# Natural feature order for the rows of the second norm, with strided reads by TensorE's transposes

## The chip, the cores and the metric

The kernel runs on one core of a Trainium2 chip. The metric is the device time of one execution in microseconds (us); the times before are the median of three runs. The engines are called as the profile calls them: PE is TensorE's matmul, PEld its weight load, DVE VectorE, ACT ScalarE, POOL GpSimd, SP SyncE.

## The reference, cut to what matters

One layer of a backbone: a mixing part (convolution and retention heads), then a channel part, a mixture of experts. What this change touches lies between the two. For each of the 640 tokens (128 context, 512 latent):

```python
x = x + g1 * m
xn = rmsnorm(x, norm_ffn_g) * (1 + sc2) + sh2
lg_group = t @ w_rg + b_rg          # t = xn as rows of 1024 features
lg_exp = t @ w_re + b_re            # top-1 group, then top-2 experts in it
hid = silu(t @ w1e) * (t @ w3e)     # for each of 32 experts
acc = acc + ge[:, None] * (hid @ w2e)
x = x + g2 * acc                    # then a last rmsnorm
```

All data is float32. A feature's place in a row of xn is free, as long as the router's and the experts' weights meet it in the same order.

## The kernel before, in words

The tokens are five tiles of 128 (tile 0 the context). `P` is 128, `D` is 1024, `KT` is 8, `NT` is 5. Each engine runs a program of its own, in the order in which it is written; semaphores join them.

**Weights and feature order.** The router's and the experts' weights lie in memory with the feature as the outer index and are loaded by "(p k) n -> p k n": partition p holds the eight features 8p to 8p+7, so that each partition gets one long piece. For step k of a product over the features, the stationary operand must therefore hold features k, 8+k, 16+k and so on. In the kernel before, DVE writes the normalised row `xn2[t]` in that order: `second_norm(t)` (lines 1568 to 1580) reads x in natural order and writes with 128 words from one element to the next, so that each block of 128 words is one k.

**Routing stage (295 to 403 us).** For each tile PE runs the output projection in two halves (`project`, line 1137), and between them the transposes of the tile before (`router_T`, line 1145: eight transposes, each loads a 128 x 128 block of `xn2` as the stationary operand), then `router` (L1154), `ranks` (L1164, L1165) and `slots` (L1174) of earlier tiles. DVE adds the residual, runs `second_norm` (L1572 to L1580; its multiplication is L1578, its addition goes through the helper at L1356), `choose` and `place`. ACT squares the rows and copies the transposes out of PSUM (L867). POOL writes every `xn2` tile to memory (`expert_in_rows`, L629).

**Expert stage (403 to 660 us).** POOL gathers the rows of two experts, 64 each, into `xe` (L633); PE transposes them (`rows_T`, L1244, eight transposes for a pair of experts, four of them in each expert's turn); DVE copies them to `xeT` (L1678). Each expert: `gate_up` (L1252, L1256), `hidden_T` (L1262), `down` (L1272). The transposes of a pair's rows stand one pair ahead, between `hidden_T` and `down` of the expert before.

**Loads of the experts.** SP loads 3 MB for each expert into five slots. The first loads wait for the output projection's two last halves (a slot becomes free), the fourth expert's for all `expert_in_rows` writes, the fifth's for the first two gathers, and every later one for the `gate_up` and `down` five experts earlier (L461, L462, L465). 

The last stage (660 to 694 us) reads both expert results of each token, adds them and normalises.

Of the kernel before, what the change touches and what calls it, by code (L numbers as in the profile page):

```python
# [7 lines left out]
P = 128  # L8
D = 1024
KT = D // P  # L10
# [61 lines left out]
ALU = mybir.AluOpType  # L72
# [59 lines left out]
def layer(nc, a, y_prompt, y_sample, new_f, new_b):  # L132
# [7 lines left out]
    with ExitStack() as ctx:  # L140
        def sb(name, shape, dt=F32):
            return ctx.enter_context(nc.sbuf_tensor(name, shape, dt))

        def sem(name):
            return ctx.enter_context(nc.semaphore(name))

        bank = [ctx.enter_context(nc.psum_tensor(f"bank{b}", [P, SL], F32)) for b in range(8)]
# [14 lines left out]
        x = sb("x", [P, NT, D])  # L162
# [22 lines left out]
        stat = sb("stat", [P, 4, NT])  # L185
# [16 lines left out]
        def k(name):  # L202
            lo, hi = CONSTS[name]
            return kept[:, lo:hi]

        ident = k("ident")
# [3 lines left out]
        q = arena_b[:, 0:2560].rearrange("p (t n) -> p t n", t=NT)  # L210
# [25 lines left out]
        rows = [arena_b[:, 2 * D * c:2 * D * c + 2 * D].rearrange("p (s n) -> p s n", s=2) for c in range(4)]  # L236
# [3 lines left out]
        xn2 = [arena_a[:, D * ((t + 3) % NT):D * ((t + 3) % NT) + D] for t in range(NT)]  # L240
# [13 lines left out]
        def tagged(t, j):  # L254
# [6 lines left out]
        xe = arena_c[:, 0:2048].rearrange("p (b n) -> p b n", b=2)  # L261
# [55 lines left out]
        ssq2_done, ms2_done, root2_done, xn2_ready, xn2T_mm, xn2T_ev, rt_mm, lg_ready = (sem(n) for n in (  # L317
            "ssq2_done", "ms2_done", "root2_done", "xn2_ready", "xn2T_mm", "xn2T_ev", "rt_mm", "lg_ready"))
# [55 lines left out]
        def bank_of(n):  # L374

            return bank[(4 + n) % 8]
# [14 lines left out]
        def conv_bank(piece, g):  # L391

            return bank[4 + g] if piece == 2 else bank[2 * g + piece % 2]
# [521 lines left out]
        def _(pe):  # L915
# [46 lines left out]
            def split_product(out, lhs, rhs, start, stop):  # L962
                pe.matmul(out, lhs[0], rhs[0], start=start, stop=False)  # L963
                pe.matmul(out, lhs[0], rhs[1], start=False, stop=False)  # L964
                return pe.matmul(out, lhs[1], rhs[0], start=False, stop=stop)  # L965


            def conv_step(piece, kt, w):

                for g in range(2):  # L970
                    cols = slice(HALF_TOK * g, HALF_TOK * g + HALF_TOK)
                    last = split_product(conv_bank(piece, g)[:, 0:HALF_TOK], w, [b[:, kt, cols] for b in (xn_hi, xn_lo)],
                                         kt == 0, kt == KT - 1)
                return last
# [27 lines left out]
            for n in range(3, CONV_PIECES):  # L1002
# [4 lines left out]
                for kt in range(KT):  # L1007
                    last = conv_step(n, kt, [b[:, kt, :] for b in w])
# [13 lines left out]
            for piece in range(CONV_PIECES, PIECES):  # L1022
# [3 lines left out]
                for t in range(NT):  # L1026
# [6 lines left out]
                    for c in range(2):  # L1033
                        kt = 2 * j + c
                        last = split_product(bank_of(n)[:, :], [b[:, kt, cols] for b in (xn_hi, xn_lo)],
                                             [b[:, c, :] for b in w], kt == 0, kt == KT - 1)
# [54 lines left out]
            for t in range(NT):  # L1091
# [8 lines left out]
                for h in range(HEADS):  # L1100
                    cols = slice(DH * h, DH * h + DH)
                    last = pe.matmul(bank[3][:, cols], sm[:, cols], v[:, t, cols], start=True, stop=(t == 0))
                    if t >= 1:
                        pe.matmul(bank[3][:, cols], qTf[t % 2][:, cols], sfw[:, cols], start=False, stop=False)
                        last = pe.matmul(bank[3][:, cols], qTb[t % 2][:, cols], sbk[:, t - 1, cols], start=False, stop=True)
# [12 lines left out]
                for h in range(HEADS):  # L1118
                    last = pe.transpose(bank[5][:, P * h:P * h + P], q[:, t, DH * h:DH * h + DH], ident)
# [20 lines left out]
            def router_T(t):  # L1140
                pe.wait_ge(xn2_ready, t + 1)
                for kt in range(KT):
                    if t >= 1 and kt % 4 == 0:
                        pe.wait_ge(xn2T_ev, 2 * t - 1 + kt // 4)
                    last = pe.transpose(bank[4 + kt // 4][:, P * (kt % 4):P * (kt % 4) + P], xn2[t][:, P * kt:P * kt + P], ident)
                    if kt % 4 == 3:
                        last.then_inc(xn2T_mm, 1)

# [30 lines left out]
            for t in range(NT):  # L1179
                project(t, 0)  # L1180
                if t >= 1:
                    router_T(t - 1)

                if t == NT - 1:
                    router(t - 1)
                project(t, 1)
                if 1 <= t < NT - 1:
                    router(t - 1)
                if t >= 3:
                    slots(t - 3)  # L1190
                if t >= 2:
                    ranks(t - 2)
# [23 lines left out]

            late_mod(0)
            router_T(NT - 1)
            slots(NT - 3)
            ranks(NT - 2)  # L1220
# [20 lines left out]
            def rows_T(p_, tiles):  # L1241

                for kt in tiles:
                    last = pe.transpose(bank[kt // 4][:, P * (kt % 4):P * (kt % 4) + P], xe[:, p_, P * kt:P * kt + P], ident)  # L1244
                    if kt % 4 == 3:
                        last.then_inc(xe_mm, 1)

# [27 lines left out]

            pe.wait_ge(xe_in[0], 16)
            rows_T(0, range(KT))
            def finish(n):

# [10 lines left out]
            for n in range(EXPERTS):  # L1290
                s, p_, pair = e_slot[n % NSLOT], n % 2, (n // 2) % 2
# [21 lines left out]
            with pe.If(count > 0):  # L1313
# [8 lines left out]
                for n in range(2 * NT):  # L1322
                    mine = tagged_ov[:, n, :].rearrange("p (m two) -> p two m", two=2)
                    for half in range(2):
                        last = pe.matmul(bank[4][BLK * half:BLK * half + BLK, 0:OVB // 2], hit_ov[:, n, :], mine[:, half, :],
                                         start=(n == 0), stop=(n == 2 * NT - 1))
# [19 lines left out]
        def _(dve):  # L1346
            steps = [0]

            def then(ins):

                steps[0] += 1
                ins.then_inc(step, 1)
                dve.wait_ge(step, steps[0])

            def tt(out, in0, in1, op):
                return dve.tensor_tensor(out, in0, in1, op)  # L1356
# [79 lines left out]
            for m in range(CB):  # L1436
                dve.wait_ge(proj_mm, CB + m + 1)
                dve.wait_ge(conv_c_ev, CB)
                for g in range(2):
                    cols = slice(HALF_TOK * g, HALF_TOK * g + HALF_TOK)  # L1440
                    last = tt(u[:, m, cols], u[:, m, cols], conv_bank(CB + m, g)[:, 0:HALF_TOK], ALU.mult)
# [5 lines left out]
            for m in range(CB):  # L1447
                for lo, hi, w in spans:
# [4 lines left out]
                                                  in1=o[:, :, 1:], op0=ALU.mult, op1=ALU.add))  # L1453
                    then(dve.scalar_tensor_tensor(out=o[:, :, 0:w - 1], in0=i_[:, :, 1:], scalar=conv_w[:, 2, m:m + 1],
                                                  in1=o[:, :, 0:w - 1], op0=ALU.mult, op1=ALU.add))
                dve.wait_ge(proj_mm, 2 * CB + m + 1)
                for g in range(2):
                    cols = slice(HALF_TOK * g, HALF_TOK * g + HALF_TOK)
                    last = tt(yconvT[:, m, cols], yconvT[:, m, cols], conv_bank(2 * CB + m, g)[:, 0:HALF_TOK], ALU.mult)
# [11 lines left out]
            for n in range(2 * (NT - 1)):  # L1471
                dst = (q, kk)[n // (NT - 1)]
                t = n % (NT - 1) + 1
# [94 lines left out]
            def second_norm(t):  # L1568
                dve.wait_ge(x1_ready, 2 * t + 2)
                dve.wait_ge(scale2_ready, 1)  # L1570
                dve.wait_ge(ssq2_done, t + 1)
                dve.tensor_scalar(stat[:, 1, t:t + 1], stat[:, 0, t:t + 1], 1.0 / D, EPS, ALU.mult, ALU.add).then_inc(ms2_done, 1)  # L1572
                dve.wait_ge(root2_done, t + 1)
                then(dve.reciprocal(stat[:, 3, t:t + 1], stat[:, 2, t:t + 1]))
                side = min(t, 1)
                as_qk = lambda r: r.rearrange("p (q k) -> p q k", q=P)
                dst = xn2[t].rearrange("p (k q) -> p q k", q=P)
                then(dve.scalar_tensor_tensor(out=dst, in0=as_qk(x[:, t, :]), scalar=stat[:, 3, t:t + 1],  # L1578
                                              in1=as_qk(rows[2][:, side, :]), op0=ALU.mult, op1=ALU.mult))
                tt(dst, dst, as_qk(rows[1][:, side, :]), ALU.add).then_inc(xn2_ready, 1)  # L1580

            def over(ap, n):

# [57 lines left out]
            for t in range(NT):  # L1641
# [9 lines left out]
                if t == 0:  # L1651
                    dve.wait_ge(rows_in[2], 16)
                    dve.wait_ge(gffn_in, 16)
                    for side in range(2):
                        last = dve.scalar_tensor_tensor(out=rows[2][:, side, :], in0=rows[2][:, side, :], scalar=1.0, in1=g_ffn,
                                                        op0=ALU.add, op1=ALU.mult)
# [163 lines left out]
            with dve.If(count > 0):  # L1820
                def ov(ins, n):
# [10 lines left out]
                                            in0=on.rearrange("p (t j) b -> p t j b", j=2)[:, :, 1, :], scalar=float(TOK), in1=second,  # L1832
                                            op0=ALU.mult, op1=ALU.add), 3)
# [6 lines left out]
                                         op1=ALU.add).then_inc(idx_ov_ready, 1)  # L1840
# [9 lines left out]
                for m in range(OVB // 2 - 1):  # L1850
                    with dve.If(count > m):
# [6 lines left out]
                        for j in range(2):  # L1858
# [4 lines left out]
                                                        scalar=g_ctx_ov[:, 2 * m + j:2 * m + j + 1], in1=gate_row[:, j, :],  # L1863
                                                        op0=ALU.mult, op1=ALU.add), 11 + 4 * m + 2 * j)
# [58 lines left out]
```

## Time and profile before

| | |
|---|---|
| time, median of three runs | 697.33 us (695.92 to 697.91) |
| profiled execution | 695.76 us, span 693.9 us |
| PE busy | 586.9 us (85%) |
| DVE busy | 311.8 us (45%) |
| ACT, POOL busy | 140.3 us, 145.3 us |
| bytes moved by DMA | 178.67 MB, mean 257 GB/s |

The span is the time from the first to the last instruction of the profiled execution; 1.86 us lie around it. The page cuts the span into 40 slices of 17.35 us. A chain of waits is the work that ended last, followed back from the end. A group of instructions is one line, engine, operation and shape. A releaser is what ended an engine's idle time.

### The profile page before, as it was taken

What the parts mean: (1) busy time and instruction counts of PE and PEld (TensorE: products, weight loads), DVE (VectorE), ACT (ScalarE), POOL (GpSimd) and SP (SyncE); (2) the same over time, 40 slices, a digit from 0 to 9 for tenths busy, and PEclk for the clock granted to TensorE, in tenths of its full rate; (3) what the DMA queues carried; (4) which work ended last, traced back from release to release, by engine and by line L of the source; (5) the groups of instructions that cost most, each with busy time, mean ns of one, the idle gap of its engine ahead of it and who ended that gap; (6) DMA issues with size and microseconds to landing.
All of it is one profiled execution on the core that took longest, in us unless ns stands there. A gap on an engine that the chain in (4) does not pass through costs nothing.

```text
span 693.9 us, 8564 instructions
## 1 busy us (share of the span) xinstructions
PE 586.9 (85%) x3496; PEld 394.9 (57%) x3496; DVE 311.8 (45%) x619; ACT 140.3 (20%) x269; POOL 145.3 (21%) x113
## 2 busy tenths in 40 slices
PE   3799999999999989899999758999888877788800
PEld 3579999888888856544554425555444433443300
DVE  1432228623602357524677636665433333334347
ACT  5334531121322333301111120111000100000012
POOL 0043642424242100020000021232222222121200
PEclk9999999999999999999999669999988999999955
DMA  7985231130330399770006899999999999999484
GB/s 276 387 296 200 71 122 53 69 122 0 122 116 6 124 369 328 256 289 30 31 31 231 361 347 400 363 422 419 419 419 420 420 419 420 420 420 420 177 317 186
DMA packets 47482, 178.67 MB, mean 257 GB/s; under 512 B 5624, under 2 KB 5800, under 8 KB 34768
## 3 DMA queue, kind: packets, MB, share of 16 engines
q1 hardware_dynamic: 39116, 155.83, 57.0%
q0 software_dynamic: 7360, 19.63, 7.8%
q10 hardware_dynamic: 964, 2.63, 1.1%
q8 instruction: 29, 0.48, 0.3%
q14 instruction: 13, 0.11, 0.0%
HBM read 170.17 MB, written 14.19 MB: 266 GB/s over the span
## 4 chain that ended last, share of the span: by engine, by line
PE 66%; DMA 21%; DVE 6%; ACT 3%; SPq 2%; issue 2%; DVEq 0%; POOLq 0%; ACTq 0%
DMA ring<-in_w_up_e 17%; PE bank L963 9%; PE bank L964 9%; PE bank L1137 9%; PE bank L965 9%; PE bank L1252 9%; PE bank L1272 4%; PE bank L922 3%; PE bank L939 2%; PE bank L1244 2%; PE bank L1154 2%; DMA ring<-expert_out_rows 1%; PE bank L1017 1%; SPq L461 1%; SPq L465 1%
## 5 line engine op out<-in xcount | busy, mean ns | idle before, releaser
L1252 PE MATMUL bank<-ring,arena_ab 128*64 128x256 f32 x416 | 104.5, 409 | 27.5 <-DMA ring<-in_w_up_e 23.7
L1256 PE MATMUL bank<-ring,arena_ab 128*64 128x256 f32 x416 | 104.6, 409 | 0.0
L1252 PEld LDWEIGHTS bank<-ring,arena_ab 128*64 128x64 f32 x416 | 59.7, 148 | 76.4 <-DMA ring<-in_w_up_e 36.8
L572 POOL TENSOR_TENSOR w_lo<-ring,w_hi 128x1024 fp32r<-128x1024 f32 x25 | 61.3, 2452 | 112.6 <-ACT w_hi L723 112.6
L643 POOL DMA_INDIRECT expert_out_rows<-arena_ab,row_out x32 | 40.1, 1254 | 130.4 <-DVE arena_ab L1356 130.4
L1356 DVE TENSOR_TENSOR arena_ab<-arena_ab,bank 64x256 f32<-64x256 f32 x32 | 19.6, 613 | 106.3 <-ACT arena_ab L879 106.2
L963 PE MATMUL bank<-xn_hi,w_hi 128*128 128x320 f32 x192 | 61.6, 321 | 3.7 <-DVE xn_lo L1356 3.6
L963 PE MATMUL bank<-w_hi,xn_hi 128*128 128x512 f32 x160 | 63.3, 396 | 0.0
L964 PE MATMUL bank<-w_lo,xn_hi 128*128 128x512 f32 x160 | 62.9, 393 | 0.0
L965 PE MATMUL bank<-w_hi,xn_lo 128*128 128x512 f32 x160 | 62.8, 392 | 0.0
L1256 PEld LDWEIGHTS bank<-ring,arena_ab 128*64 128x64 f32 x416 | 59.7, 148 | 0.0
L964 PE MATMUL bank<-xn_lo,w_hi 128*128 128x320 f32 x192 | 59.4, 310 | 0.0
L965 PE MATMUL bank<-xn_hi,w_lo 128*128 128x320 f32 x192 | 59.3, 309 | 0.0
L879 ACT ACTIVATE arena_ab<-bank 64x256 f32<-64x256 f32 x32 | 12.0, 376 | 224.6 <-PE bank L1256 224.6
L1272 PE MATMUL bank<-ring,arena_ab 128*64 128x512 f32 x208 | 50.4, 605 | 1.4 <-ACT arena_ab L883 1.4
L723 ACT ACTIVATE w_hi<-ring 128x1024 fp32r<-128x1024 f32 x25 | 26.5, 1062 | 114.1 <-PE bank L965 114.1
L963 PEld LDWEIGHTS bank<-xn_hi,w_hi 128*128 128x128 f32 x192 | 36.5, 190 | 6.7 <-issue 5.0
L1356 DVE TENSOR_TENSOR arena_ab<-bank,arena_ab 128x512 f32<-128x512 f32 x37 | 25.5, 690 | 27.9 <-PE bank L1272 27.8
L1137 PE MATMUL bank<-ring,arena_cd 128*128 128x512 f32 x80 | 36.4, 597 | 1.3 <-ACT arena_ab L847 1.3
L965 PEld LDWEIGHTS bank<-xn_hi,w_lo 128*128 128x128 f32 x192 | 36.6, 191 | 0.0
L964 PEld LDWEIGHTS bank<-xn_lo,w_hi 128*128 128x128 f32 x192 | 36.5, 190 | 0.0
L1137 PE MATMUL bank<-ring,arena_ab 128*128 128x512 f32 x80 | 36.0, 592 | 0.0
(235 smaller groups left out, 903.3 us busy)
## 6 DMA issues: line engine op xcount, KB each, us to landing
ring<-in_w_gate_e SPq DMA_DIRECT2D x26, 1024.0 KB, 26.3
ring<-in_w_up_e SPq DMA_DIRECT2D x26, 1024.0 KB, 28.0
ring<-in_w_down_e SPq DMA_DIRECT2D x26, 1024.0 KB, 26.7
ring<-in_w_ada SPq DMA_DIRECT2D x11, 2048.0 KB, 12.8
ring<-in_w_in SPq DMA_DIRECT2D x6, 2048.0 KB, 8.2
arena_ab<-in_w_gate_e SPq DMA_DIRECT2D x6, 1024.0 KB, 25.8
arena_ab<-in_w_up_e SPq DMA_DIRECT2D x6, 1024.0 KB, 27.5
arena_ab<-in_w_down_e SPq DMA_DIRECT2D x6, 1024.0 KB, 26.2
```

The source lines that it names most:

```text
L572: pool.tensor_tensor(as_piece(w_lo[p_ % 2], p_), piece_of(w, p_), as_piece(w_hi[p_ % 2], p_), ALU.subtract).then_inc(w_lo_ready, 1)
L643: pool.indirect_dma_start(half_rows, bass.IndirectOffsetOnAxis(ap=column, axis=0), ysb[:, p_, :], None, bounds_check=2 * 2 * TOK - 1, oob_ ...
L723: act.activation(as_piece(w_hi[piece % 2], piece), piece_of(w, piece), ACT.Copy).then_inc(w_hi_ready, 1)
L922: last = pe.matmul(out[32 * j:32 * j + 32, :], cs[:, kt, :], w[:, kt, :], start=(kt < 4), stop=(kt >= 4))
L963: pe.matmul(out, lhs[0], rhs[0], start=start, stop=False)
L964: pe.matmul(out, lhs[0], rhs[1], start=False, stop=False)
L965: return pe.matmul(out, lhs[1], rhs[0], start=False, stop=stop)
L1137: last = pe.matmul(bank[n % 4][:, :], lhs, w[:, kt, :], start=(kt == 0), stop=(kt == KT - 1))
L1252: pe.matmul(bank[2 + p_][0:BLK, 0:DE], lhs, w_gate(s)[:, kt, :], start=(kt == 0), stop=(kt == KT - 1))
L1256: last = pe.matmul(bank[2 + p_][BLK:2 * BLK, 0:DE], lhs, w_up(s)[:, kt, :], start=(kt == 0), stop=(kt == KT - 1))
L1272: last = pe.matmul(bank[6 + p_][BLK * half:BLK * half + BLK, :], hidT[:, p_, c, :], w_down(s)[:, c, SL * half:SL * half + SL], start=(c == ...
L1356: return dve.tensor_tensor(out, in0, in1, op)
```

## The change

DVE writes the normalised rows in natural feature order: both of its operations on a tile read and write consecutive words. The rows go to memory and come back by the gather in that order. PE's transposes in `router_T` and `rows_T` take, for step k, every eighth word of a row from word k on, so that the transposed blocks hold what they held before. Nothing else is changed: the number of instructions, the bytes moved and the waits are the same.

```diff
@@ router_T
-                    last = pe.transpose(bank[4 + kt // 4][:, P * (kt % 4):P * (kt % 4) + P], xn2[t][:, P * kt:P * kt + P], ident)
+                    last = pe.transpose(bank[4 + kt // 4][:, P * (kt % 4):P * (kt % 4) + P], xn2[t][:, kt:D:KT], ident)
@@ rows_T
-                    last = pe.transpose(bank[kt // 4][:, P * (kt % 4):P * (kt % 4) + P], xe[:, p_, P * kt:P * kt + P], ident)
+                    last = pe.transpose(bank[kt // 4][:, P * (kt % 4):P * (kt % 4) + P], xe[:, p_, kt:D:KT], ident)
@@ second_norm
                 side = min(t, 1)
-                as_qk = lambda r: r.rearrange("p (q k) -> p q k", q=P)
-                dst = xn2[t].rearrange("p (k q) -> p q k", q=P)
-                then(dve.scalar_tensor_tensor(out=dst, in0=as_qk(x[:, t, :]), scalar=stat[:, 3, t:t + 1],
-                                              in1=as_qk(rows[2][:, side, :]), op0=ALU.mult, op1=ALU.mult))
-                tt(dst, dst, as_qk(rows[1][:, side, :]), ALU.add).then_inc(xn2_ready, 1)
+                then(dve.scalar_tensor_tensor(out=xn2[t], in0=x[:, t, :], scalar=stat[:, 3, t:t + 1],
+                                              in1=rows[2][:, side, :], op0=ALU.mult, op1=ALU.mult))
+                tt(xn2[t], xn2[t], rows[1][:, side, :], ALU.add).then_inc(xn2_ready, 1)
```

## Rows read from the trace of the kernel before

**Rows 1.** Page, 40 slices of the span: DMA share in tenths, GB/s
```profile
DMA  7985231130330399770006899999999999999484
GB/s 276 387 296 200 71 122 53 69 122 0 122 116 6 124 369 328 256 289 30 31 31 231 361 347 400 363 422 419 419 419 420 420 419 420 420 420 420 177 317 186
```

**Rows 2.** Chain of waits, 313 to 435 us: start, duration (us), what
```profile
313.98 2.00 DVE arena_ab L1578
...
351.42 0.87 PE bank L1145 x8
...
382.71 1.98 DVE arena_ab L1578
...
404.04 5.32 DMA arena_cd<-expert_in_rows,idx
...
409.41 1.98 PE bank L1244 x8
...
418.95 0.59 PE bank L1244 x4
...
425.86 2.60 issue
...
434.09 0.59 PE bank L1244 x4
```

**Rows 3.** Timeline: transposes of tiles 0, 2 and 4; idle before and releaser
```profile
317.96 1.09 PE L1145 MATMUL bank<-kept,arena_ab 128*128 128x128 f32 x8 [1.66 <-DVE arena_ab L1356]
...
351.25 0.80 PEld L1145 LDWEIGHTS bank<-kept,arena_ab 128*128 128x128 f32 x7 [0.29 <-issue]
...
386.65 1.57 PEld L1145 LDWEIGHTS bank<-kept,arena_ab 128*128 128x128 f32 x8 [5.49 <-DVE arena_ab L1356]
386.66 1.97 PE L1145 MATMUL bank<-kept,arena_ab 128*128 128x128 f32 x8 [4.58 <-DVE arena_ab L1356]
```

**Rows 4.** Groups by shape, DVE: busy us, mean ns | idle before
```profile
L1578 DVE SCALAR_TENSOR_TENSOR arena_ab<-x,stat,arena_ab 128x1024 f32<-128x1024 f32 x5 | 10.0, 1995 | 0.2
L1356 DVE TENSOR_TENSOR arena_ab<-arena_ab 128x1024 f32<-128x1024 f32 x5 | 9.6, 1919 | 0.2
L1887 DVE SCALAR_TENSOR_TENSOR ring<-x,stat,arena_ab 128x1024 f32<-128x1024 f32 x5 | 6.4, 1284 | 0.5 <-DMA out<-ring 0.4
L1356 DVE TENSOR_TENSOR x<-x,ring 128x1024 f32<-128x1024 f32 x5 | 6.1, 1224 | 0.2
```

**Rows 5.** The same view: sums over 32 words, strided (L1620) and consecutive
```profile
L1636 DVE TENSOR_REDUCE arena_cd<-arena_cd 128x1 f32<-128x32 f32 x10 | 1.9, 186 | 0.3
...
L1620 DVE TENSOR_REDUCE arena_cd<-arena_cd 128x8 f32<-128x32 f32 x5 | 1.0, 206 | 0.2
```

**Rows 6.** Stretches: length, busy us of each engine, granted clock, DMA share, GB/s
```profile
382.00:386.60 4.60, 0.07 (x4) 0.00 (x0) 4.18 (x5) 0.69 (x2) 0.00 (x0) 0.86 1.01 426
386.60:399.00 12.40, 12.34 (x62) 7.97 (x62) 7.20 (x42) 1.78 (x3) 0.53 (x1) 0.50 0.85 336
...
425.80:428.40 2.60, 0.06 (x2) 0.00 (x0) 2.40 (x7) 0.00 (x0) 0.06 (x1) 1.00 0.90 284
430.00:433.00 3.00, 3.00 (x18) 2.10 (x16) 0.27 (x1) 0.00 (x0) 1.18 (x1) 0.50 1.03 429
436.00:438.00 2.00, 2.00 (x20) 1.21 (x18) 1.37 (x3) 0.00 (x0) 0.00 (x0) 1.00 0.34 80
...
452.00:498.00 46.00, 46.00 (x344) 25.52 (x340) 25.07 (x43) 5.22 (x16) 13.22 (x12) 1.00 1.02 420
```

**Rows 7.** Timeline of SP's queue: issues of expert loads
```profile
368.82 0.34 SPq L461 DMA_DIRECT2D ring<-in_w_gate_e  x1
...
436.58 0.33 SPq L465 DMA_DIRECT2D ring<-in_w_down_e  x1
...
468.09 0.33 SPq L465 DMA_DIRECT2D ring<-in_w_down_e  x1
...
474.26 0.33 SPq L465 DMA_DIRECT2D ring<-in_w_down_e  x1
```

**Rows 8.** Line L633, the sixteen gathers of expert rows: time to landing
```profile
DMA to landing us min/median/max: 4.4/8.5/9.8
```

## The prediction

> **What bounds the kernel now.** I read the page's slices first: from the 26th on (about 434 us) the DMA engines are full at 419 to 420 GB/s, up to the 36th or 37th, some 640 us [rows 1]. That is the loading of the experts. One expert is 3 MB, so it takes 3.146 MB / 420 GB/s = 7.5 us; SP's issues, which follow PE's progress, are 6.17 us apart at 468 to 474 us [rows 7]. PE is thus faster than the loads in the middle of the expert stage, and the end of that stage is the time at which the load queue was last empty, plus the bytes that were left. The last such hole is at 436 to 438 us, where the DMA share is 0.34 and 80 GB/s are moved [rows 6]; it ends with the issue at 436.58 us, which waits for PE's `down` of the second expert [rows 7]. So whatever moves the issue at 436.58 us moves the end by as much, and work that PE gains or loses after it, below 7.5 - 6.17 = 1.3 us an expert, moves nothing.
>
> Then the chain of waits up to there. DVE's norm of tile 0 is on it (313.98 us), then PE through the routing stage without a gap that DVE ends (the transposes of tile 2 stand in it as PE's own work), then DVE's norm of tile 4 (382.71), PE, the first gather (404.04, 5.32 us), the eight transposes of the first pair (409.41), four in the first expert's turn (418.95), a pause of PE of 2.60 us at 425.86, and four more at 434.09 [rows 2]. The timeline says how long PE stood: 1.66 us before tile 0's transposes and 4.58 us before tile 4's, both for DVE [rows 3].
>
> **DVE's part, removed.** In the strided form the multiplication takes 1995 ns and the addition 1919 ns. Nearest forms with consecutive words: the last norm's multiplication (same operands, 1284 ns) and an addition of two 128x1024 operands (1224 ns) [rows 4]. A tile gains 711 + 695 = 1406 ns, five tiles 7.0 us. For tiles 1 to 3 it lies beside PE's projections and is worth nothing. For tile 0 it is on the path: PE is ready 1.66 us before DVE, so all of 1.41 us counts. For tile 4 again 1.41 us. Together -2.82 us, the whole gain to be had.
>
> **PE's part, added.** No weight load of the kernel before reads with a stride, so the price must be bounded. What a transpose costs now: the seven weight loads in 0.80 us, each lasting 0.14 us, start (0.80 - 0.14) / 6 = 0.11 us apart [rows 3], and eight transposes take 0.87 us on the chain, 0.109 us each [rows 2]: the transposes go at the pace of their weight loads, with nothing in between to hide a longer load. At the clock of 0.50 at 386.6 to 399 us [rows 6] eight take 1.97 us [rows 3].
>
> [...] Below nothing is excluded, since no word less is loaded. For the other end I take what DVE pays. A sum over 32 words takes 186 ns with consecutive words and 206 ns where every eighth word is read, the stride of this change: 20 / 32 = 0.62 ns a word, though it has eight results instead of one [rows 5]. The norm's two operations give 711 / 1024 = 0.69 and 695 / 1024 = 0.68 ns a word for a stride of 128 words [rows 4]. I take 0.69 ns: 128 words, 0.088 us a transpose. If a strided word has a time of its own and not a surcharge, it is about 1224 / 1024 + 0.69 = 1.9 ns less the fixed part of the operation (186 ns for a sum over 32 words, so some 0.15 us or 0.15 ns a word), 1.7 ns: 0.22 us a transpose, 0.11 us more. So 0 to 0.11 us, and I take 0.088, since two views of DVE agree on it; that PE's port behaves as DVE's is the open point.
>
> [...]
>
> **The sum up to 436.58 us, at 0.088 us a transpose.**
> - Tile 0: DVE -1.41.
> - Transposes of tiles 0 to 3: 32 x 0.088 = +2.82. SP's first expert load (368.82 us [rows 7]) is then issued 1.41 us later.
> - Tile 4: DVE -1.41.
> - Transposes of tile 4: 8 at half clock. A load there has 1.57 / 8 = 0.20 us [rows 3], 1.5 ns a word, close to the 1.7 ns of a strided word, so the surcharge may vanish or stay: 0 to 0.70, I take +0.35. The list of rows to gather is ready at +0.35.
> - The gather runs among loads of the experts that were issued at +1.41. Its 5.32 us are near the shortest of the sixteen, 4.4 us [rows 8], so it follows its own issue more than the queue; between +0.35 and +1.41 I take +0.9.
> - First pair's eight transposes, again at half clock: +0.35.
> - The four at 418.95: DVE copies them out and then works without a pause until PE may go on at 428.46 us: +0.35.
> - The next four (423.41): PE then stands 2.60 us for that DVE work; DVE is busy 2.40 us of it [rows 6]. They are free as long as they cost under 2.60 us.
> - The four at 434.09: +0.35.
>
> Sum +0.9 + 3 x 0.35 = +1.95 us.
>
> **After it.** Four transposes an expert add 0.35 us to 6.17, 6.52 us, still under the loads' 7.5. The last experts have no transposes in their turn, so the end of the stage and the last stage stay. DVE's writes to memory, the gathers and the results are the same bytes. So +1.95 us at the end: the profiled execution of 695.76 us becomes 697.7 us. That execution is 1.57 us under the median of the three runs, 697.33, to which the time below refers: 699.3 us.
>
> With 0 us a transpose: the list is ready at -2.82, the loads come at -1.41, the gather between, and the sum is -2.1 us: 695.2 us. With 0.11 us: 32 x 0.11 - 2.82 = +0.7 at the list, +2.1 at the loads, the gather at +1.4, then little for the eight at half clock and 2 x 0.44: about +2.5 us, 699.8 us. About 0.3% (2.1 us) is what a measurement of this kernel can tell from no change, so the forecast lies just inside.
>
> **The rivals.**
> - *Strided weight loads are free.* For it: nothing in the trace shows PE paying for any pattern, and the load may be paced by the array. Against: DVE pays for reads and for writes alike [rows 4, 5], at a pace of about 1 ns a word, and PE at full clock wants a word every 0.85 ns, faster still. 695.2 us.
> - *A strided load costs more than DVE's surcharge, and the transposes replace DVE as what the routing stage waits for.* The place is the 32 transposes of tiles 0 to 3 between the projections, which no wait covers. It decides from about 0.09 us a transpose, where the sum passes +2.1 us. For it: the 0.11 us pitch leaves a load no slack at all [rows 3]. At twice DVE's price, 0.176 us: the loads at 32 x 0.176 - 1.41 = +4.2, the list at 5.6 - 2.8 + 1.4 = +4.2, then 1.4 + 0.7 + 0.7 for the pairs, +7.0 us: 704.3 us. Only from 1.3 / 4 = 0.33 us a transpose would the whole expert stage go at PE's pace.
> [...]
>
> **How the numbers follow.** Forecast 0.50, free loads 0.28, dearer loads 0.13, clock kept 0.09. The forecast's own bounds (+1 to +2.6 us) and the spread of the three runs (2 us from lowest to highest) put 0.28 of its 0.50 inside 0.3% and 0.22 above. Free loads: 0.16 faster, 0.12 inside. Dearer loads: all slower. Clock kept: 0.04 faster, 0.05 inside. So faster 0.20, within 0.3% 0.45, slower 0.35. The range reaches down to the free loads' time and up to the beginning of the dearer ones, 694.9 to 703.0 us; it leaves out about half of the dearer loads and some of the free ones' spread.
>
> **What the profile after would show.** L1578 near 1.28 us and the addition near 1.22 us; PE's wait before tile 0 near 0.3 us. The weight loads of L1145 at full clock 0.2 us apart and eight transposes in about 1.6 us on the chain (0.87 if they are free). SP's first expert load 1.4 us later (1.4 earlier if free). The hole near 436 us still there, moved by the sum. In the full stretch 452 to 498 us [rows 6] SP's issues 6.5 us apart, DMA still at 420 GB/s. The prediction is wrong if a transpose has another pitch, if DMA no longer fills that stretch, or if the gather doesn't follow the list.

## The result and the profile after

| | before | changed |
|---|---|---|
| time, median of ten runs | 697.13 us (694.75 to 699.27) | 693.79 us (691.96 to 695.06) |
| profiled execution, span | 693.9 us | 692.9 us |
| DVE busy | 311.8 us | 304.9 us |
| PEld busy | 394.9 us | 398.1 us |

The ratio to the kernel before is 0.9948, 95% interval 0.9934 to 0.9963: 3.6 us faster (2.6 to 4.6). The forecast was 699.3 us with a range of 694.9 to 703.0, so the change went the other way and just out of the range. It lies beside the first rival, free strided loads (695.2 us).

DVE first. Groups by shape of the changed kernel, busy us and mean ns of one behind the bars; L1576 and the first L1356 are the norm's multiplication and addition:

```profile
L1576 DVE SCALAR_TENSOR_TENSOR arena_ab<-x,stat,arena_ab 128x1024 f32<-128x1024 f32 x5 | 6.4, 1285 | 0.2
...
L1885 DVE SCALAR_TENSOR_TENSOR ring<-x,stat,arena_ab 128x1024 f32<-128x1024 f32 x5 | 6.4, 1285 | 0.5 <-DMA out<-ring 0.4
...
L1356 DVE TENSOR_TENSOR arena_ab<-arena_ab 128x1024 f32<-128x1024 f32 x5 | 6.1, 1225 | 0.2
```

Both are what the nearest consecutive forms said [rows 4]: 1995 - 1285 = 710 ns and 1919 - 1225 = 694 ns.

Then PE. The timeline of the changed kernel, with the idle time before an operation in brackets: the transposes of tile 0, the weight loads of tile 2 (seven of the eight), the transposes of tile 4:

```profile
316.16 1.15 PE L1145 MATMUL bank<-kept,arena_ab 128*128 128x128 f32 x8 [0.28 <-DVE arena_ab L1356]
...
349.53 0.86 PEld L1145 LDWEIGHTS bank<-kept,arena_ab 128*128 128x128 f32 x7 [0.24 <-issue]
...
385.30 1.97 PE L1145 MATMUL bank<-kept,arena_ab 128*128 128x128 f32 x8 [3.23 <-DVE arena_ab L1356]
```

Against [rows 3]: PE waits 0.28 instead of 1.66 us before tile 0, and 3.23 instead of 4.58 us before tile 4, 1.38 and 1.35 us gained. A weight load lasts 0.19 instead of 0.14 us, but they start (0.86 - 0.19) / 6 = 0.11 us apart, as before. The chain of waits, with start and duration:

```profile
313.56 1.30 DVE arena_ab L1576
...
349.69 0.89 PE bank L1145 x8
...
370.67 8.66 PE bank L1137 x16
...
382.70 1.29 DVE arena_ab L1576
...
402.94 5.15 DMA arena_cd<-expert_in_rows,idx
...
408.14 1.99 PE bank L1244 x8
...
424.95 2.55 issue
```

Eight transposes take 0.89 instead of 0.87 us [rows 2]. The 8.66 us are an accident of the clock (below): the same sixteen products took 6.96 us before. In stretches of the changed kernel (length, busy times, then granted clock, DMA share, GB/s):

```profile
370.70:374.50 3.80, 3.80 (x6) 1.48 (x6) 3.23 (x19) 0.00 (x0) 0.00 (x0) 0.55 1.01 420
...
385.30:398.00 12.70, 12.70 (x63) 7.99 (x63) 7.16 (x41) 1.78 (x3) 0.53 (x1) 0.50 0.99 385
...
429.70:433.10 3.40, 3.40 (x26) 2.06 (x24) 1.29 (x2) 0.65 (x2) 0.51 (x1) 1.00 1.01 419
434.00:436.00 2.00, 2.00 (x22) 1.35 (x20) 1.93 (x4) 0.00 (x0) 0.51 (x1) 1.00 1.00 334
```

The granted clock was 0.50 at 371 to 374 us, where it had been 1.00 before, and 1.00 at 430 to 433 us, where it had been 0.50 [rows 6]. Such stretches fall differently in the two executions. The first cost PE 8.66 - 6.96 = 1.7 us, more than tile 0 had given, so tile 4's norm began no earlier than before (382.70 and 382.71 us). The second gave as much back: PE's pause ended at 427.50 us, 0.96 us earlier than before, and the issue that ended the last hole came earlier by 2.6 us:

```profile
434.00 0.33 SPq L465 DMA_DIRECT2D ring<-in_w_down_e  x1
```

It was at 436.58 us before [rows 7]. That the 2.6 us lie near the two terms of the norm is therefore partly luck of this execution. The last expert's first product came at 647.63 instead of 649.80 us, and the last stage from there took 45.3 instead of 44.1 us; so the spans of the two profiles differ by only 1.0 us, the medians by 3.3 us. The steps below are read from single stages, the gain from the medians.

### The profile page after: what moved, and what is told of

It reads as the page before. It is cut to its first block, busy times and chain, and to the rows that moved or that the text cites. A ratio compares the mean times of both kernels' runs of the same rounds, so it can differ in the third digit from the quotient of the medians.

```text
span 692.9 us, 8564 instructions
## 1 busy us (share of the span) xinstructions
PE 588.9 (85%) x3496; PEld 398.1 (57%) x3496; DVE 304.9 (44%) x619; ACT 140.2 (20%) x269; POOL 145.3 (21%) x113
## 4 chain that ended last, share of the span: by engine, by line
PE 67%; DMA 21%; DVE 5%; ACT 3%; SPq 2%; issue 2%; DVEq 0%; POOLq 0%; ACTq 0%
DMA ring<-in_w_up_e 17%; PE bank L963 9%; PE bank L1137 9%; PE bank L964 9%; PE bank L965 9%; PE bank L1252 9%; PE bank L1272 4%; PE bank L922 3%; PE bank L939 2%; PE bank L1244 2%; PE bank L1154 2%; DMA ring<-expert_out_rows 1%; PE bank L1017 1%; SPq L461 1%; PE bank L1086 1%
## 5 line engine op out<-in xcount | busy, mean ns | idle before, releaser
L1356 DVE TENSOR_TENSOR arena_ab<-arena_ab,bank 64x256 f32<-64x256 f32 x32 | 19.4, 607 | 103.8 <-ACT arena_ab L879 103.7
L1137 PE MATMUL bank<-ring,arena_cd 128*128 128x512 f32 x80 | 38.1, 621 | 1.3 <-ACT arena_ab L847 1.3
L1356 DVE TENSOR_TENSOR arena_ab<-bank,arena_ab 128x512 f32<-128x512 f32 x37 | 25.6, 691 | 29.6 <-PE bank L1272 27.6
```

The lines of the kernel that those rows point to most:

```text
L1137: last = pe.matmul(bank[n % 4][:, :], lhs, w[:, kt, :], start=(kt == 0), stop=(kt == KT - 1))
```

## The experiments

Two theories stood after the result. **A:** the gain is the shorter norm before tiles 0 and 4, and strided loads cost next to nothing. **B:** it came from PE's side (the reads, the clock) or from DVE's lighter load as a whole. Within A it was open why the loads cost nothing: because their pace is the same with any stride (**A1**), or because something hides it (**A2**). Times are ratios to the kernel before, run on the same chip in turn. The edits are shown cut, with "..." or a capital name such as TILES where something is left out.

**The norm made slow again, on all tiles, on 1 to 3, on 0 and 4.** PE's strided reads stay in all three.

```diff
+                order = (lambda r: r.rearrange("p (q k) -> p k q", k=KT)) if t in TILES else (lambda r: r)
-                then(dve.scalar_tensor_tensor(out=xn2[t], in0=x[:, t, :], ...
+                then(dve.scalar_tensor_tensor(out=order(xn2[t]), in0=order(x[:, t, :]), ...
-                tt(xn2[t], xn2[t], rows[1][:, side, :], ALU.add)
+                tt(order(xn2[t]), order(xn2[t]), order(rows[1][:, side, :]), ALU.add)
```

> The changed kernel, with DVE's two operations of the second norm made slow again: they go through the row with eight words from one element to the next, on all operands, and leave it in natural order. PE's strided transposes stay. Theory A (the gain is DVE's shorter norm before tiles 0 and 4, PE's strided loads cost next to nothing): about the time of the kernel before, 697 us, ratio to it 0.998 to 1.002, if the two operations again take about 1.9 us; each 1 us that they take more or less counts twice (tiles 0 and 4) for each operation. Theory B (the gain came from PE's side, the reads or the clock): it stays near the changed kernel, 694 us, ratio 0.995.

> As the kernel with the slow norm, but slow for tiles 1, 2 and 3 only. Theory A: these lie beside PE's projections, so the time is that of the changed kernel, 694 us, ratio to the kernel before 0.995. Rival (DVE's load as a whole counts, also through the choosing and placing that stand behind the norm): three fifths of the gain are lost, ratio about 0.998.

> As the kernel with the slow norm, but slow for tiles 0 and 4 only. Theory A: the whole gain is lost, ratio to the kernel before 0.998 to 1.002. Rival (DVE's load as a whole): two fifths are lost, ratio about 0.997.

Measured: all tiles 1.0017 (0.9995 to 1.0039), tiles 1 to 3 0.9964 (0.9947 to 0.9982), tiles 0 and 4 1.0007 (0.9980 to 1.0033). The price of the slow form, from the groups of the kernel with all five tiles slow:

```profile
L1577 DVE SCALAR_TENSOR_TENSOR arena_ab<-x,stat,arena_ab 128x1024 f32<-128x1024 f32 x5 | 10.4, 2087 | 0.2
L1356 DVE TENSOR_TENSOR arena_ab<-arena_ab 128x1024 f32<-128x1024 f32 x5 | 10.1, 2011 | 0.2
```

They are 92 ns each above the form before, and the gain is gone. It goes as well with tiles 0 and 4 alone, where DVE's load as a whole would have left 0.997. With tiles 1 to 3 the interval takes in the changed kernel's 0.9948, but the rival's 0.998 too, so that run alone doesn't decide. PE's waits in the profiles do. Tile 4's transposes with all tiles slow, then with tiles 1 to 3 slow:

```profile
388.39 1.97 PE L1145 MATMUL bank<-kept,arena_ab 128*128 128x128 f32 x8 [4.76 <-DVE arena_ab L1356]
...
385.22 1.16 PE L1145 MATMUL bank<-kept,arena_ab 128*128 128x128 f32 x8 [3.23 <-DVE arena_ab L1356]
```

Before tile 0 PE waits 1.86 and 0.28 us; with tiles 0 and 4 slow it is 1.86 and 4.77 us, and before tiles 1 to 3 PE doesn't wait in any of the three. So the gain is DVE's, and only where PE waits for it. B is out for this part.

**Consecutive reads in the experts' transposes.** The router's reads stay strided; the experts then work on features in another order than their weights have, so this kernel computes something else in the same instructions.

```diff
-  last = pe.transpose(..., xe[:, p_, kt:D:KT], ident)
+  last = pe.transpose(..., xe[:, p_, P * kt:P * kt + P], ident)
```

> The changed kernel with consecutive reads in the experts' transposes again; the router's stay strided, so that the routing is the reference's, and the experts work on features in another order than their weights have. Theory A: 128 transposes gain a few ns each and the first of each run of four some 50 ns, of which three runs lie before the load queue's last hole: ratio to the kernel before as the changed kernel, 0.995, lower by at most 0.0005. If strided loads cost what the forecast said (0.088 us), the sixteen transposes before the hole would give 1 us or more: 0.9935.

Measured 0.9939 (0.9917 to 0.9960). The interval holds both expectations, so this run alone doesn't settle the price; the probes do.

**Probes of the weight load by itself.** PE has nothing to do in the last stage, so probes stand there; the longer total times of these kernels are the probes'.

```diff
...
+            for stride in (1, 8, 16):      # then products with 1, 2, 4, 8, 12
+                for n in range(12):
+                    pe.transpose(bank[1][:, 0:P], probe[:, ...:stride], ident)
```

> The changed kernel with probes on PE behind the last expert, beside the last stage: 24 products to raise the clock, then runs of 12 transposes with 1, 8 and 16 words between the elements of the stationary block, then runs of 12 products with 16 moving columns and 1, 2, 4, 8 and 12 words. With 16 columns the weight loads alone set the pace. Theory A1 (a strided load only takes longer from start to end, loads overlap and their pace is the same): transposes 0.11 us apart in all three runs, products 0.21 us apart (two loads each) in all five. Theory A2 (strided loads come at a slower pace too, which the transposes' own columns hide): transposes 0.11 us apart, products slower from a stride of 8 words on, up to 0.44 us apart (two loads of 0.22). The forecast's theory (0.088 us more a load): transposes 0.2 us apart.

All 36 transposes, with 1, 8 and 16 words from element to element, stand in one row of the timeline of PEld:

```profile
677.83 0.14 PEld L1349 LDWEIGHTS bank<-kept,arena_ab 128*128 128x128 f32 x1 [0.24 <-issue]
678.26 3.97 PEld L1349 LDWEIGHTS bank<-kept,arena_ab 128*128 128x128 f32 x35 [0.29 <-issue]
```

(3.97 - 0.19) / 34 = 0.111 us apart: the forecast's 0.2 us is out. Taken by stride the loads start 0.109, 0.111 and 0.113 us apart. The products of 16 columns ran into a stretch with a granted clock of 0.50, from 688.0 us on, before the larger strides came, so they were run again, each run behind six wide products; there the clock was 1.00 from 669 to 711 us.

```diff
...
+            for stride in (8, 1, 4, 12, 2, 8):
+                for n in range(6):
+                    pe.matmul(bank[0][:, :], ident, arena_ab[:, 0:SL], start=True, stop=True)
+                for n in range(4):
+                    pe.matmul(bank[2][:, 0:16], probe[:, ...:stride], ident[:, 0:16], start=True, stop=True)
```

> The changed kernel with probes on PE behind the last expert: six runs of six wide products, which keep the clock up, each followed by four products of 16 columns whose stationary block is read with 8, 1, 4, 12, 2 and again 8 words from element to element. Each such product has two weight loads, and nothing else that takes time. Theory A1 (a strided load takes longer from start to end, but loads overlap and come at nearly the same pace): 112 ns apart with 1 word, 115 to 125 ns with 8, so at most 13 ns a load. Theory A2 (strided loads come at a slower pace that the transposes' own columns hide): 150 ns and more with 8 words. The forecast's price would be 200 ns.

Eight weight loads a run, two for each product; the first starts 0.43 us ahead, beside the last wide product, and with 1 and 2 words it has a row of its own. In the order of the strides:

```profile
674.60 2.17 PEld L1351 LDWEIGHTS bank<-kept,arena_ab 128*128 128x128 f32 x8 [0.24 <-issue]
...
681.52 0.19 PEld L1351 LDWEIGHTS bank<-kept,arena_ab 128*128 128x128 f32 x1 [0.24 <-issue]
681.95 0.86 PEld L1351 LDWEIGHTS bank<-kept,arena_ab 128*128 128x128 f32 x7 [0.24 <-issue]
...
687.57 2.14 PEld L1351 LDWEIGHTS bank<-kept,arena_ab 128*128 128x128 f32 x8 [0.24 <-issue]
...
694.46 2.37 PEld L1351 LDWEIGHTS bank<-kept,arena_ab 128*128 128x128 f32 x8 [0.24 <-issue]
...
701.59 0.20 PEld L1351 LDWEIGHTS bank<-kept,arena_ab 128*128 128x128 f32 x1 [0.24 <-issue]
702.01 0.91 PEld L1351 LDWEIGHTS bank<-kept,arena_ab 128*128 128x128 f32 x7 [0.23 <-issue]
```

Consecutive: (0.86 - 0.19) / 6 = 0.112 us apart. Two words: 0.118. Eight, where a load lasts 0.33 us: (2.17 - 0.43 - 0.33) / 6 = 0.235, four 0.23, twelve 0.26. From four words on a strided load does come at half the pace (it had been expected from eight on): A1 falls, and the question became where that goes in a transpose.

**Transposes of 64 rows,** which have the same load of 128 words and only 64 moving columns.

```diff
...
+                for n in range(8):
+                    pe.transpose(bank[1][:, 0:BLK], probe[0:BLK, ...:stride], ident[0:BLK, 0:BLK])
```

> The changed kernel with probes on PE behind the last expert: six runs of six wide products, which keep the clock up, each followed by eight transposes of 64 rows by 128 words, read with 8, 1, 4, 2, 16 and again 8 words from element to element. Such a transpose has a weight load of 128 words but only 64 moving columns, half of those of the kernel's own. Theory A2 (a strided load comes at half the pace of a consecutive one, as in the products of 16 columns, where it was 237 against 112 ns; in a transpose of 128 columns the columns' own 109 ns hide it): about 60 ns apart with 1 and 2 words, 105 to 120 ns with 4, 8 and 16. Theory A1 (loads of transposes have the same pace with any stride): the same spacing, 55 to 65 ns, in all six runs.

Eight loads a run, with 8, 1, 4, 2 and 16 words:

```profile
674.67 0.96 PEld L1351 LDWEIGHTS bank<-kept,arena_ab 64*128 64x128 f32 x8 [0.76 <-issue]
...
681.05 0.57 PEld L1351 LDWEIGHTS bank<-kept,arena_ab 64*128 64x128 f32 x8 [0.76 <-issue]
...
687.03 1.03 PEld L1351 LDWEIGHTS bank<-kept,arena_ab 64*128 64x128 f32 x8 [0.76 <-issue]
...
693.48 1.03 PEld L1351 LDWEIGHTS bank<-kept,arena_ab 64*128 64x128 f32 x8 [0.76 <-issue]
...
699.92 0.97 PEld L1351 LDWEIGHTS bank<-kept,arena_ab 64*128 64x128 f32 x8 [0.76 <-issue]
```

Consecutive: (0.57 - 0.14) / 7 = 0.061 us apart. Eight words, where a load lasts 0.20 us: (0.96 - 0.20) / 7 = 0.109; sixteen 0.11, four and two 0.117 to 0.12, though 0.06 had been expected with two. That is A2: a strided load costs 0.048 us more, 0.061 to 0.109, and a transpose of 128 columns takes 0.109 us for its columns anyway. (The 0.061 us may be the pace of the 64 columns, as half of 0.109 is 0.055; the load's own pace is then below it and its surcharge above 0.048 us.)

The probe halves the rows together with the columns, so that loads of 64 rows might be the faster ones. Against it stand the first two loads of the experts' transposes, which have 128 rows, and of which the second starts before the 128 columns of the first transpose have passed; kernel before, then changed kernel:

```profile
423.33 0.20 PEld L1244 LDWEIGHTS bank<-kept,arena_cd 128*128 128x128 f32 x2
...
422.37 0.30 PEld L1244 LDWEIGHTS bank<-kept,arena_cd 128*128 128x128 f32 x2
```

Each lasts 0.14 us before and up to 0.21 us after, so the second starts 0.06 us behind the first with consecutive words and 0.09 us with strided ones: the same load, without the columns.

The cover is used up to the last nanoseconds: in the kernel the strided transposes of the router stand 0.11 us apart, and eight of them are longer by 0.02 us. At the start of a run there is no cover: the experts' four transposes take 0.64 us in the changed kernel's chain and took 0.59 us before [rows 2].

**The clock kept up.** Nine products into a bank that nobody reads, in PE's pause before tile 4's transposes; twelve while PE waits for the first gather; both.

```diff
             late_mod(0)
+            for n in range(9):
+                pe.matmul(bank[3][:, 0:384], ident, kept[:, 0:384], start=True, stop=True)
             router_T(NT - 1)
...
+            for n in range(12):
+                pe.matmul(bank[2][:, 0:384], ident, kept[:, 0:384], start=True, stop=True)
             pe.wait_ge(xe_in[0], 16)
```

> The changed kernel with nine products of 384 columns on PE, into a bank that nobody reads, in its pause before tile 4's transposes. Clock theory (the pause is what drops the clock from 385 to 399 us): the clock stays at 1.0 up to 399 us, tile 4's transposes take 0.9 instead of 2.0 us and its router products 1.7 instead of 3.4, the list of rows is ready 2 to 3 us earlier and the end comes 1 to 2.5 us earlier: ratio to the kernel before 0.991 to 0.994. Rival (the gather then waits behind the loads, or the clock falls anyway): ratio 0.995 as the changed kernel.

> The changed kernel with twelve such products while PE waits for the first gather. [...] Rival (the end hangs on the loads that were issued before the gather): 0.995.

> Both fillings. [...] Rival (loads bound): no more than the better of the two alone.

Measured 0.9953 (0.9931 to 0.9974), 0.9970 (0.9956 to 0.9985), 0.9974 (0.9952 to 0.9996): none better than the changed kernel. The stretches of the kernel with both fillings show that the clock did stay in its profile:

```profile
382.00:386.00 4.00, 4.00 (x14) 2.33 (x13) 3.00 (x12) 0.00 (x0) 0.53 (x1) 1.00 1.00 418
386.00:399.00 13.00, 9.52 (x79) 5.92 (x78) 7.81 (x44) 2.86 (x5) 0.03 (x1) 0.98 1.00 393
```

In its one profile the issue after the second expert came at 430.78 us, 3.2 us before the changed kernel's 434.00, and that execution took 690.37 us, the fastest of twelve; the slowest took 698.54, and the median is 694.69. It isn't a typical one: its mean granted clock was 0.965, that of the eleven others 0.949 to 0.956. Where they lost it isn't seen in a profile and stays open.

The fillings were also longer than the pauses. With the pause filled, the products, the end of DVE's norm of tile 4 and the transposes:

```profile
380.29 6.07 PE L1219 MATMUL bank<-kept 128*128 128x384 f32 x18
...
382.32 1.22 DVE L1358 TENSOR_TENSOR arena_ab<-arena_ab 128x1024 f32<-128x1024 f32 x1
...
386.20 1.05 PE L1145 MATMUL bank<-kept,arena_ab 128*128 128x128 f32 x8
```

DVE was done at 383.54 us, so the filling itself held the transposes back by 2.7 us. With the gather's wait filled, the gather's instruction, the products and the first pair's transposes:

```profile
400.73 1.07 POOL L633 DMA_INDIRECT arena_cd<-expert_in_rows,idx  x1 [16.58 <-DVE idx L1674]
...
400.75 8.86 PE L1277 MATMUL bank<-kept 128*128 128x384 f32 x24
...
409.44 1.05 PE L1244 MATMUL bank<-kept,arena_cd 128*128 128x128 f32 x8
```

The gather landed after 5.6 us, at 406.3 us, and the filling held PE for 3.1 us more. So these runs show that the clock can be kept up there, and that such fillings don't pay; they don't show what the clock alone would be worth.

**The counting moved behind the hole.** PE's pause of 2.55 us in the third expert's turn waits for DVE's counting for the overflow; it is moved to turns where PE waits for loads anyway. The changed kernel was run again beside it.

```diff
-                if n == 0:
+                if n == 12:
                     overflow_counts()
-                elif n == 2:
+                elif n == 14:
                     overflow_slots()
-                elif n == 4:
+                elif n == 16:
                     block_table()
```

> The changed kernel with DVE's three blocks of counting for the overflow moved from the turns of experts 0, 2 and 4 to those of 12, 14 and 16, where PE waits for the loads anyway. PE's pause of 2.55 us in the third expert's turn goes. Theory H (the end is the issue that ends the last hole of the load queue, plus a fixed 213 us to the last gate and up load): the issue after the second expert comes 2 to 2.5 us earlier and the end with it, ratio to the kernel before 0.991 to 0.993. Rival (the loads are the bound from 411 us on, the hole only moves): ratio 0.995 as the changed kernel.

> The changed kernel itself, for a comparison on the same chip: ratio to the kernel before 0.993 to 0.997.

Measured 0.9921 (0.9898 to 0.9944) against 0.9946 (0.9925 to 0.9967) for the changed kernel: 692.84 and 694.14 us. The point is as theory H had it, though the intervals overlap; it is the lowest ratio here. The issue came at 431.06 us, 2.9 us earlier, but the stretch behind it holds no hole any more:

```profile
431.00:433.00 2.00, 2.00 (x22) 1.29 (x18) 1.84 (x3) 0.00 (x0) 0.44 (x1) 1.00 1.02 424
```

So the gain should be at most the rest of a hole (434 to 436 us of the changed kernel moved 334 GB/s, where 420 are full); that is argued, not shown. From that issue to the last expert's first product it took 213.2 us in the kernel before, 213.6 in the changed one, 213.3, 212.9 and 215.4 with the slow norms, 212.9 with the experts' consecutive reads, 212.8, 213.1 and 213.1 with the pause, the gather's wait and both filled, 215.3 in the changed kernel again, and 216.0 here, where the hole was gone.

## Why the prediction was wrong

**The term that failed** is the price of a strided transpose: 0.088 us forecast, (0.89 - 0.87) / 8 = 0.0025 us measured. With 32 of them before the loads it made +2.82 us of a forecast of +1.95; measured it is 32 x 0.0025, under 0.1 us, and some 0.06 us for tile 0, whose eight took 1.15 instead of 1.09 us. The further terms of 0.35 us, four of them, came to nothing at half clock (1.97 us for tile 4's eight, as before; 1.99 and 1.98 us for the first pair's) and to 0.05 us for each four of the experts' transposes (0.64 and 0.59 us).

The step behind it is the sentence "the transposes go at the pace of their weight loads, with nothing in between to hide a longer load". The 0.109 us are the pace of the 128 moving columns; the loads alone would come at most 0.061 us apart, and 0.048 us lay free. A transposing product whose columns are half as many stood in the trace before. In the timeline of PEld of the kernel before, two loads of 128 words for `hidden_T`:

```profile
433.75 0.20 PEld L1262 LDWEIGHTS bank<-kept,arena_ab 64*128 64x128 f32 x2 [0.39 <-issue]
```

Each lasts 0.14 us, so they start 0.06 us apart. That row would have set the cover, and the forecast's 0.088 us would have become 0.061 + 0.088 - 0.109 = 0.04 us. In the forecast's own steps the list is then ready at -2.82 + 32 x 0.04 + 0.16 = -1.4 us, the loads come at -0.1, the gather halfway at about -0.75, and 3 x 0.16 us follow: some -0.3 us instead of +1.95.

DVE's surcharge as a measure for PE was of the right kind, but not one size: 0.69 ns a word forecast, 0.048 us / 128 = 0.38 ns measured for a transpose's load and (0.235 - 0.112) us / 128 = 0.96 ns for a product's. The probes give 0.112 to 0.235 us for the loads of a product with eight words. With two words the loads of a transpose already came 0.118 instead of 0.061 us apart, and those of a product 0.118 instead of 0.112; with four, a product's came 0.23 us apart. That a price exists says nothing of the time as long as something as long runs beside it, here the 0.109 us of the columns.

**DVE's part was right.** 1406 ns a tile forecast, 710 + 694 = 1404 ns measured; that only tiles 0 and 4 count is shown by the slow norms, and PE's waits there shrank by 1.38 + 1.35 = 2.7 us, where 2.8 had been forecast.

**The sum for free loads** was -2.1 us, the measurement is -3.6 (-2.6 to -4.6). Part of it is the gather, for which half of tile 4's gain was written off to the loads in the queue: it took 5.15 us after 5.32 and so followed the list of rows whole; that makes -2.8 us, inside the interval. The range's lower end, 694.9 us, lay 0.3 us under that rival's own time, although the rival had a chance of 0.28 and a spread of the runs of 2 us: it was cut too close.

**The clock.** The chance of 0.09 for a clock that is kept up by the shorter pause didn't come true: before tile 4's transposes PE waited 3.23 us instead of 4.58 [rows 3], and the clock was 0.50 at 385 to 398 us, as it had been at 386.6 to 399 us [rows 6]; in all nine profiles with a pause of 3.23 or 3.24 us it was 0.50 at 388 to 390 us. What a kept clock would be worth stays open: with the clock kept up no fewer us were measured, but the fillings themselves cost 2.7 and 3.1 us.

**After the hole.** SP's issues went from 6.17 to 6.23 us apart at 466 to 472 us, the loads stayed at 420 GB/s; the 0.06 us an expert that the strided reads add there are free, as forecast. That the end moves with the issue at the hole held within 0.8 us in eight of the eleven profiles above. In the three others the end came 2 to 3 us later; in one of them the hole was gone, in the other two the reason stays open.

## What to carry to other kernels

A row of products that start 0.11 us apart has two paces, the weight load's (at most 0.061 us here) and the moving columns' (0.109 us), and the slower one is seen: before pricing a slower load, look for a product of the same load with fewer columns and read the load's own pace there. A layout change that costs one engine a stride and saves another a stride is worth what each of them has free at that place: here DVE's 1.4 us a tile stood on the path of two tiles of five, and PE's 0.048 us a transpose lay under its columns. That holds for this place only: the probe's products of 16 columns paid the stride in full, 0.235 instead of 0.112 us a load.

## What the runs showed of the hardware

- A strided weight load of 128 words: 0.109 to 0.12 us instead of 0.061 for transposes of 64 rows of float32 data, 0.23 to 0.26 us instead of 0.112 for each of the two loads of a float32 product with four to twelve words between the elements; two words cost the product 0.118 us.
- The strided pace of the products' loads didn't follow the clock: in the first probe the products with four, eight and twelve words ran at a granted clock of 0.50 (from 688 us on), and their loads came 0.233, 0.238 and 0.267 us apart; at 1.00, in the second, it was 0.23, 0.235 and 0.26 us. In tile 4's transposes at 0.50 no price is seen: 1.57 us for eight loads in both kernels.
- In the first probe's products of 16 columns PE was busy throughout, and the granted clock still fell from 1.00 to 0.50; stretches of half a microsecond, PE, PEld, clock, DMA share, GB/s:

```profile
687.50:688.00 0.50, 0.50 (x6) 0.50 (x5) 0.97 0.98 401
688.00:688.50 0.50, 0.50 (x4) 0.50 (x3) 0.50 0.35 139
```
